# The hyena's first chunk turned and transformed ahead of the first attention scores, its steps begun two turns earlier

## The reference

```python
# differential attention, 4 heads, two softmaxes each
s = jnp.einsum('bqhmd,bkhmd->bhmqk', q, k).astype(F32) * DIFF_SCALE
p = jax.nn.softmax(s, axis=-1)
attn = p[:, :, 0] - lam * p[:, :, 1]
return jnp.einsum('bhqk,bkhe->bqhe', attn.astype(v.dtype), v)

# order-2 hyena: two long convolutions by FFT over 1024 latent tokens, 512 channels
uf = jnp.fft.rfft(u.astype(F32), n=2 * L, axis=1)
y = jnp.fft.irfft(uf * kf, n=2 * L, axis=1)[:, :L]
...
z = x1 * _fft_long_conv(v, kf[:, 0], bias[0])
return x2 * _fft_long_conv(z, kf[:, 1], bias[1])
```

## Time and profile before

| | |
|---|---|
| median of 3 runs | 3959.79 us (3956.76 to 3960.09) |
| the profiled execution's own time | 3963.66 us |
| its span in the profile | 3961.7 us |
| mean granted TensorE clock | 0.945 of full speed |
| busy: PE, DVE, ACT, POOL | 86%, 64%, 27%, 25% |

### The profile page before, as it was taken

How to read it: one execution, slowest core, us unless ns; L and a number is a source line. 1 busy time by engine, 2 the same in 40 slices (tenths; PEclk the granted TensorE clock), 3 DMA queues, 4 the chain that set the end, 5 groups by cost and what they waited for, 6 DMA issues and landing times. The chain is left out here.

```text
span 3961.7 us, 48983 instructions
## 1 busy us (share of the span) xinstructions
PE 3408.4 (86%) x18212; PEld 2768.9 (70%) x18212; DVE 2544.2 (64%) x4960; ACT 1087.1 (27%) x1979; POOL 997.2 (25%) x702
## 2 busy tenths in 40 slices
PE   7999999999758886886897799999999688858798
PEld 2787888888647775554684577888887577745477
DVE  4134557766459996785564324567775599968765
ACT  2111122211334444231310211222211455523321
POOL 4233333332101111210221513433343011122121
PEclk8999999999879998998998899999999799979999
DMA  5254223223173221433624255322322633133442
GB/s 208 66 157 133 89 72 101 90 84 95 41 204 90 61 76 45 141 100 111 183 85 177 89 110 176 98 83 92 98 93 61 198 87 90 39 107 105 125 140 73
DMA packets 414895, 423.35 MB, mean 107 GB/s; under 512 B 57040, under 2 KB 351440, under 8 KB 413506
## 3 DMA queue, kind: packets, MB, share of 16 engines
q1 hardware_dynamic: 368676, 315.22, 27.6%
q10 hardware_dynamic: 45984, 105.01, 7.6%
HBM read 287.76 MB, written 124.01 MB: 104 GB/s over the span
## 5 line engine op out<-in xcount | busy, mean ns | idle before, releaser
L751 PE MATMUL l_p_acc<-l_u_hi,l_w_hi 128*128 128x512 f32 (+1 forms) x2208 | 605.4, 376 | 24.5 <-ACT l_p_stg L815 9.7
L751 PE MATMUL l_p_acc<-l_u_hi,l_w_lo 128*128 128x512 f32 (+1 forms) x2208 | 588.0, 368 | 0.0
L751 PE MATMUL l_p_acc<-l_u_lo,l_w_hi 128*128 128x512 f32 (+1 forms) x2208 | 587.6, 367 | 0.0
L751 PEld LDWEIGHTS l_p_acc<-l_u_hi,l_w_hi 128*128 128x128 f32 x2208 | 384.0, 190 | 101.3 <-issue 27.3
L751 PEld LDWEIGHTS l_p_acc<-l_u_lo,l_w_hi 128*128 128x128 f32 x2208 | 381.4, 189 | 71.7
L751 PEld LDWEIGHTS l_p_acc<-l_u_hi,l_w_lo 128*128 128x128 f32 x2208 | 381.3, 189 | 71.8
L664 POOL TENSOR_TENSOR l_w_hi<-l_wt,l_p_zero 128x1024 fp32r<-128x1024 f32 x100 | 202.2, 2022 | 910.7 <-PE l_p_acc L751 753.2
L1518 PE MATMUL l_at_pS<-l_at_k_hi,l_at_q 128*128 128x512 f32 (+1 forms) x400 | 166.8, 417 | 138.2 <-ACT l_at_prob L1634 86.2
L666 POOL TENSOR_TENSOR l_w_lo<-l_wt,l_w_hi 128x1024 fp32r<-128x1024 f32 x100 | 262.8, 2628 | 7.8
L2453 PE MATMUL l_o_pA<-l_o_w_hi,l_o_o_hi 128*128 128x512 f32 x576 | 224.4, 408 | 40.8 <-DVE l_o_o_lo L2563 30.5
L1737 DVE TENSOR_REDUCE l_at_nmax<-l_at_pS 128x1 f32<-128x1280 f32 (+1 forms) x144 | 197.2, 1369 | 88.2 <-PE l_at_pS L1519 83.1
(11 more groups left out here) (330 smaller groups left out, 7102.9 us busy)
## 6 DMA issues: line engine op xcount, KB each, us to landing
l_wt<-w_in SPq DMA_DIRECT2D x104, 512.0 KB, 3.9
l_n_wa<-w_ada SPq DMA_DIRECT2D x10, 2048.0 KB, 16.7
kf_d<-l_p_R SPq DMA_DIRECT2D x72, 256.0 KB, 3.4
xbc_d<-l_p_fin ACTq DMA_DIRECT2D x28, 640.0 KB, 2.9
l_at_K<-kf_d SPq DMA_DIRECT2D x64, 256.0 KB, 2.9
l_o_rows<-w_out SPq DMA_DIRECT2D x32, 512.0 KB, 5.0
l_o_oT<-o_d SPq DMA_DIRECT2D x16, 1024.0 KB, 7.0
qk_d<-l_p_late ACTq DMA_DIRECT2D x12, 1280.0 KB, 4.6
```

The source lines that it names most:

```text
L751: mm = pe.matmul(acc[:, a:a + w], (w_hi, w_lo)[wp][m % 2][:, k], (u_hi, u_lo)[up][:, k, t0 + c:t0 + c + w], start=(k == n == 0), stop=(k = ...
```

## The change

It does five things. The transfer of u of chunk 0 is issued ahead of SP's part of head 0's queries and keys. TensorE and ScalarE turn and copy both its halves (`TURN_AHEAD`) before their loops begin. VectorE does all five levels of `forth(0)` before its first maximum. The halves of chunk 1 stand in turns 0 and 1, where chunk 0's first half and chunk 1 stood. And `FIRST_STEP` is 1, so that step n stands in turn n + 1, with `forth` and `backs` of all other phases two turns earlier too; the steps fill turns 1 to 32. The numbers of instructions and of bytes stay as they are.

```diff
-TURN_IN = {0: (0, 1), 1: (2, 3), 2: (4,), 3: (5,), 4: (6,), 5: (7,), 6: (8,), 7: (9,), 8: (10,), 9: (11,), 10: (12,), 11: (13,), 12: (14,), 13: (15,)}
-FIRST_STEP = 3
+TURN_AHEAD = (0, 1)
+TURN_IN = {0: (2,), 1: (3,), 2: (4,), 3: (5,), 4: (6,), 5: (7,), 6: (8,), 7: (9,), 8: (10,), 9: (11,), 10: (12,), 11: (13,), 12: (14,), 13: (15,)}
+FIRST_STEP = 1
...
     def rows_before(i):
-        return sum(len(TURN_IN.get(t, ())) for t in range(i))
+        return len(TURN_AHEAD) + sum(len(TURN_IN.get(t, ())) for t in range(i))
...
                 sp.dma_start(lv[:], lam_vecs.partition_broadcast(P)).then_inc(lam_in, 16)
+                sp.dma_start(flat(u, 0), chunk_rows(0)).then_inc(u_in[0], 16)
                 for m in range(2):
                     load_scores(sp, 0, m, 0)
-                sp.dma_start(flat(u, 0), chunk_rows(0)).then_inc(u_in[0], 16)
...
+                for r in TURN_AHEAD:
+                    turn_rows(r)
                 for i in range(NI):
                     n = step_of(i)
...
+                for r in TURN_AHEAD:
+                    copy_rows(r)
                 for i in range(NI + 1):
...
+                forth(0, 0, 5)
                 for i in range(NI):
                     if i < NU:
                         maximum(i, 0)
...
-                    if part >= 2 and 0 <= p + 1 < len(phases):
+                    if part >= 2 and 0 <= p and p + 1 < len(phases):
                         forth(p + 1, *((0, 2), (2, 5))[part - 2])
```

## The result

| | before | after |
|---|---|---|
| median (runs on the same chip) | 3959.94 us | 3984.73 us (3974.77 to 3988.67) |
| ratio, 95% interval | 1 | 1.0056 [1.0044, 1.0068] |
| the profiled execution's own time | 3963.66 us | 3986.51 us |
| span | 3961.7 us | 3984.3 us |
| stage of the first layer | 478.5 us | 495.2 us |

The kernel is 24.8 us slower with the change; 3984.7 was measured where 3979 was forecast, near the upper end of the forecast's range. A stage is counted from the issue of its first fetch (`l_at_lv`) to that of the next stage's first. The two stages lose 16.7 and 6.9 us, all others together gain 1.0.

A forecast was written before the change was run, and what follows sets the result against it. VectorE's work was taken to set the length of turns with hyena steps, and transfers to hold up the stage's start; +16.0 us (first layer) and +2.8 (second) gave +18.8, so 3979 us, range 3964 to 3986.

The forecast's parts named there:

- the two rows on the products of step 2: Start of both layers: these products start 0.8 us earlier in the first layer and 7.7 us earlier in the second.
- the two rows on the turns behind them: Turns after step 2's products: two added full turns cost 16.8 us in the first layer, 24.1 in the second.
- The transfer of u ahead: Stage start, SP's queue: keys end last, all later fetches shift by 1.0 us; bounds 0 and 2 us.
- Turning and `forth(0)` ahead at nothing: Before the first maximum: 9.2 us of butterflies cost nothing, covered by TensorE's wait for keys and chunk 1.
- 22.1 us from `forward(0)` to turn 3's maximum: Early turns, both layers: steps 0 and 1 take 22.1 us as before, giving turn 3's maximum at 1155.0 in the first.
- A time much under 22.1 us: Turns of steps 0 and 1: taking much less than 22.1 us together would show the forecast wrong.
- The spectrum of step 2: Turn 3, both layers: its queue place is unmoved, so VectorE waits 6.7 and 5.5 us before the products.
- The rival without that wait: Turn 3: the spectrum lands in time; +9.3 us first layer, -2.7 second, together +6.6, 3966; chance 0.17.
- Two more turns without steps: First layer's end: seven full turns without a step instead of five, +16.8 us; bounds 15.4 and 18.2.
- The second layer's end: Behind turn 31's maximum: the remainder to the last store shrinks from 49.8 to 36.2 us, 13.6 less.
- TensorE slow after the stalls: Turns behind the stalls at low clock cost 2 to 4 us each: +25 to +35, 3985 to 3995; chance 0.08.
- The rule weighed: Stage start: by the skill's busiest-engine rule, moving VectorE's work into its gap is good; the forecast's sum disagreed.

The follow-up runs named there:

- Experiment 1: Changed kernel with FIRST_STEP back at 3: chunk 0 fetched, turned and transformed ahead, steps in their old turns; ratio 1.0001 to the kernel before.
- experiment 3: Changed kernel with head 1's transfers and chunks 2 and 3 issued over turns 1 to 5, behind each turn's spectrum; ratio 1.0015 to the kernel before.
- 4: Kernel before with head 1's transfers and chunks 2 and 3 spread over turns 1 to 5, as a control; ratio 1.0001.
- 6: Changed kernel with chunk 1's u, matrices and first two spectra ahead of head 0's values, bulk transfers not spread; ratio 1.0059 to the kernel before.
- 5: Changed kernel with transfers spread over turns 1 to 5, and chunk 1's u, matrices, first two spectra ahead of head 0's values; ratio 0.9993 to before.
- 12: Changed kernel with FIRST_STEP 2, transfers spread, head transfers ahead of SP's GpSimd wait, matrices ahead of head 0's values; 3957.02 us, ratio 0.9981 to before.
- experiment 10: Kernel before with chunk 0's u fetched and turned ahead, other halves one per turn, transfers spread, matrices ahead of head 0's values; ratio 0.9991.
- experiment 2: Changed kernel with FIRST_STEP = 2, so that step n stands in turn n + 2; ratio 1.0053 to the kernel before.

## Why the prediction was right, by its steps

The sign, the mechanism and its place were right, and the size nearly: +18.8 us forecast, +22.6 in the span, +24.8 in the medians. In part that is luck: the two rows on the products of step 2 were 5.4 us too low together, and the two rows on the turns behind them 3.1 too high. Term by term, places counted from the stage's start:

| term | forecast | measured |
|---|---|---|
| first layer, products of step 2 | -0.8 | +1.2 |
| first layer, two more turns without steps | +16.8 | +15.4 |
| second layer, products of step 2 | -7.7 | -4.3 |
| second layer, from there to turn 31 | +24.1 | +22.4 |
| second layer, behind turn 31's maximum, to the last store | -13.6 | -12.2 |
| second layer, last store to the next stage | 0 | +1.0 |

*The transfer of u ahead* is the mis-sized term. "All later fetches shift by that 1.0 us" measured 2.9 us for the third spectrum in the first layer and 4.2 in the second. I read 1.0 us from the rows in which u landed behind the keys. Ahead of them its 512 KB take 2.6 us (an estimate) at the 201 GB/s of the first layer's start:

```profile
1093.00:1116.00 23.00, 3.02 (x10) 1.93 (x10) 8.95 (x37) 2.68 (x4) 3.41 (x6) 0.50 0.81 201
```

And head 0's values are issued 23.1 us after the stage's start instead of 20.3 (2.7 later in the second layer). The rest of the second layer's 4.2 stays open. The bound above, 2 us, was too low as well. This one term accounts for both rows on the products of step 2: 1.9 of the 2.0 us there, 3.2 of the 3.4.

*Turning and `forth(0)` ahead at nothing*: holds. VectorE ends them at 1116.3, the last keys land at 1116.1, and turn 1 waits until 1127.2 for chunk 1 anyhow. Experiment 1 puts the whole part ahead, the shift included, at 6.0 us in the stages.

*22.1 us from `forward(0)` to turn 3's maximum*: 22.4 in the second layer (3132.52 to 3154.90), but 17.8 in the first (1133.06 to 1150.87). Unit 1 is a small one there; the turns that I took the 22.1 from were full. A time much under 22.1 us was named as a sign of being wrong; here it shows no more than that the small unit was overlooked. It cost nothing, since the wait for the spectrum took up the difference: 11.0 us where 6.7 was forecast, against 4.8 for 5.5 in the second layer.

*The spectrum of step 2*: right, and shown by 3 (the wait goes, and 16 of the 25 us with it) and by 4 and 6. The rival without that wait said 3966; experiment 3 is that case and has 1.0015, 3966 too. That the number fits so well is luck: by layers the rival said +9.3 and -2.7, and the stages of 3 have +6.4 and +3.1.

*Two more turns without steps*: 7.7 each, at the lower bound (read from turns 37 and 38; the first layer behind the products of step 2 has 15.5 in all). *The second layer's end*: 37.6 us behind turn 31's maximum for the 36.2 forecast.

*TensorE slow after the stalls*, a rival whose 3985 to 3995 begins where the measured time lies: TensorE comes out of the wait partly slow. Over turn 3 the granted clock is 0.70 on average, so part of it was at 1.2 GHz and part at 2.4, with TensorE busy 10.6 of 22.5 us:

```profile
1151.00:1173.50 22.50, 10.60 (x61) 9.43 (x61) 10.51 (x25) 6.59 (x17) 0.00 (x0) 0.70 0.66 207
```

From the products to the next maximum it takes 8.2 us instead of 7.9 in the first layer (1165.31 to 1173.47), so 0.3 us and not 2 to 4, and 7.6 instead of 7.9 in the second. So the time fits this rival by number only.

*The rule weighed.* The Trainium skill, "Perfetto Trace Analysis", section "Optimization Strategy", says to find the gaps of the engine in question and what blocks it there, and then to make that start sooner or end faster. The forecast took the change to be a good one by this rule, and that was read wrongly: the change puts VectorE's work into its gap, but none of the transfers that ended the gap, chunk 1, `inv` and the third spectrum, starts sooner by it. This trace agrees with the rule as it is written. With only the work moved, the gap came back as waits of 11.0 and 4.8 us for the spectrum; with those fetches issued sooner (5, 12) the loss was gone, and 12 was faster than before.

## What to carry to other kernels

Whoever moves a step forward must move its fetches forward too: on a queue served in order the bulk ahead of a small urgent fetch sets when the step can run, and making anything else earlier only lengthens that wait. Moving work to an idle start also leaves bare turns at the other end; here each costs 7.7 us, 2.5 of them with VectorE idle, since attention alone can't fill it, so the gain at the start must beat that. And every reordering has its own last one: the transfer that gives way (the head's values in experiment 10, u's bytes ahead of the keys in the change) has to be followed to who needs it.

## What the runs showed of the hardware

The issue of a transfer is not always short. The last of the fourteen transfers of a head, its gates (`l_at_g`), held SP for 16.27 us in the change's first layer (15.14 before) and for 8.38 us in turn 23 of experiment 2, where its neighbours took 0.60. So a fetch can be late twice, by an issue that comes late and by the list ahead of it: the third spectrum was issued 58.6 us behind the stage's start and landed 13.6 us later in the change, and 46.1 and 3.0 us in experiment 3, where it stood ahead of that head. What in the queue holds the issue up, no run here shows.

For 27 us of the second layer's start DMA was busy without a pause: its share is 1.04 from 3116 to 3143, at 325 GB/s, while VectorE works 9.6 us of it. Where the engines wait in such a stretch, the order of the fetches decides who waits.
